# Expert sums gathered from the output, added on VectorE and scattered back, in place of an accumulating scatter into a scratch

## The chip, the core and the metric

The kernel runs on one core of a Trainium2 chip. The metric is device time in microseconds (us) of one execution, the median of some runs; lower is better. Engines are named as in the profile: PE is TensorE, DVE is VectorE, ACT is ScalarE, POOL is GpSimd, SP is SyncE. SPq and POOLq are instructions that these engines issue to the DMA engines.

## The reference

One layer of a diffusion backbone over 1024 tokens of 1024 channels: three mixers, a merge into the residual stream, and then a mixture of 16 experts with two experts for each token. Only its end is touched by the change. With `x` the stream after the mixers and `h2` its normalised and modulated copy:

```
x = x + g1 * merge_branches(...)
h2 = modulate(x, norm2_w, sh2, sc2)
expert, gate = route(h2, router_w, router_bias)        # two experts of a token, weights that sum to 1
y[e] = (silu(h @ w_gate[e]) * (h @ w_up[e])) @ w_down[e]   # for the tokens of expert e
out = x + g2 * sum over the two experts of (gate * y[expert])
```

All tensors are float32. Each expert has three 1024x1024 matrices, 12 MB, so the stage reads 192 MB of weights.

## The kernel before, in words

The stages run one after the other: the mixers, `project_out` (output projection, residual `x1`, second norm, router scores), `route` (which token sits in which slot) and `experts`. A block is 32 tokens of one expert; an expert has at least two blocks, and with these inputs there are 73. `k.block_row` holds the row numbers of each block. Empty slots of an expert's last block point at spare rows behind the 1024 real ones.

A block's data lies as 128 partitions of 256 columns: a token's row is cut into four quarters, and partition 32 j + r holds quarter j of slot r. So one indirect DMA of GpSimd moves 128 rows of 1 KB, each to or from a place of its own in DRAM.

`project_out` writes `x1` to the scratch tensor `sum_rows` (L2267) and the normalised rows to `xn_rows`; both scratch tensors have 32 spare rows, which are filled once (L2271). In `experts`, for block b:

- GpSimd gathers the block's rows of `xn_rows` into `rows` (L2574), ahead of their use.
- VectorE turns and modulates them into `rowsT` (`turn_rows`, L2583 to L2586).
- TensorE forms gate and up products (`p_gate_up`, L2697), then, for the block before, the down product (`p_y`, L2711).
- ScalarE and VectorE form the hidden values and turn them (`hide`, L2734 to L2753).
- VectorE scales `p_y` by the token's weight and by g2 into `y` (`store`, L2761), and counts it in the semaphore `y_stored`. TensorE's next `p_y` waits for that count.
- GpSimd scatters `y` with an accumulating indirect DMA: each row is added to its row of `sum_rows` (L2664). It counts in `added`. The next block's scatter and the next write of `y` wait for it, since two blocks may add to the same token.

SyncE streams the weights into a ring of 20 units of 1 MB (two half units of 512 KB); an expert needs 12. A unit is loaded again once the last block of its expert has used it (`gate_ups` and `downs` against the end of the expert), so loads come in bursts as an expert ends. All these queues share the 16 DMA engines.

When all scatters have landed, `finish` copies `sum_rows` to the output with four DMAs of 1 MB (L2792).

Of the kernel before, what the change touches and what calls it, by code (L numbers as in the profile page):

```python
# [22 lines left out]
F32 = mybir.dt.float32  # L23
# [2201 lines left out]
def project_out(k):  # L2225
# [4 lines left out]
    with ExitStack() as st:  # L2230
# [25 lines left out]
        with nc.Block() as block:  # L2256
            @block.sync
            def _(sp):
                credit(s, sp, per, "load_x", "load_x1_out", "load_xn_out")
                with sp.Fori(0, SEQ // P) as it:  # L2260
                    ps = Pass(s, sp, it, per)
                    src = dr["x"][0, ds(it * P, P), :]
                    d1, dn = dr["sums"][ds(it * P, P), :], dr["xn"][ds(it * P, P), :]
                    ps.after_last("x1")
                    sp.dma_start(x[:], src).then_inc(s("load_x"), 16)
                    ps.after("x1")
                    sp.dma_start(d1, x1[:]).then_inc(s("load_x1_out"), 16)  # L2267
                    ps.after("in_quarters")
                    sp.dma_start(dn, xq[:]).then_inc(s("load_xn_out"), 16)
                for name in ("sums", "xn"):  # L2270
                    sp.dma_start(dr[name][SEQ:SEQ + BLK, :], dr["x"][0, 0:BLK, :]).then_inc(s("spare_rows"), 16)  # L2271
                sp.wait_ge(s("load_x1_out"), 16 * (SEQ // P + 1))
                sp.wait_ge(s("load_xn_out"), 16 * (SEQ // P + 1))
                sp.wait_ge(s("spare_rows"), 32)
# [327 lines left out]
def experts(k):  # L2602
# [4 lines left out]
    with ExitStack() as st:  # L2607
# [8 lines left out]
        y = k.sb(st, "y", [P, W])  # L2616
        p_gu = k.ps(st, "p_gate_up", [P, 512])
        p_y = k.ps(st, "p_y", [P, 512])

        def quarters(name):  # L2620
            return dr[name].rearrange("t (i n) -> (t i) n", i=4)
# [10 lines left out]
        with nc.Block() as block:  # L2632
# [16 lines left out]
            def _(pool):  # L2649
# [6 lines left out]
                def add_rows(b):  # L2656

                    if not isinstance(b, int) or b:
                        pool.wait_ge(s("added"), b * 16)
                    nc.gpsimd.tensor_copy(row_y[:, :], k.block_row[:, ds(b, 1)]).then_inc(s("row_y"), 1)  # L2660
                    pool.wait_ge(s("row_y"), b + 1)
                    pool.wait_ge(s("y_stored"), b + 2)
                    pool.sem_inc(s("adds_begun"), 1)
                    nc.gpsimd.indirect_dma_start(quarters("sums"), bass.IndirectOffsetOnAxis(ap=row_y[:, 0:1], axis=0),  # L2664
                                                 y[:, :], None, compute_op=ALU.add).then_inc(s("added"), 16)

                n = blocks(pool)
                for b in (1, 2, 3):
# [3 lines left out]
                with pool.Fori(2, n) as b:  # L2672
                    pool.wait_ge(s("x_taken"), b + 2)
                    gather(b + 2)
                    add_rows(b + -1)
                add_rows(last_block(pool))
                pool.wait_ge(s("gathered"), pool.snap(n * 16 + 32))
                pool.wait_ge(s("added"), pool.snap(n * 16))
                pool.sem_inc(s("all_added"), 1)
# [57 lines left out]
            def _(dve):  # L2737
                ch = Chain(dve, s("dve_steps"))
                dve.sem_inc(s("hidden"), 1)  # L2739
# [15 lines left out]
                def store(b, ch):  # L2755

                    dve.wait_ge(s("downs"), b * 4 + 8)
                    if not isinstance(b, int) or b:
                        dve.wait_ge(s("added"), b * 16)
                    ch.run(nc.vector.tensor_copy(weight[:, :], k.block_weight[:, ds(b, 1)]))  # L2760
                    nc.vector.scalar_tensor_tensor(y[:, :], p_y[:, 0:W], weight[:, 0:1], g2[:, :], ALU.mult, ALU.mult) \  # L2761
                        .then_inc(s("y_stored"), 1)
# [8 lines left out]
                with dve.Fori(2, n) as b:  # L2771
                    ch.enter(b + -2, 3)
# [5 lines left out]


def finish(k):  # L2780

    nc, dr = k.nc, k.dram
    PARTS = 4
    with ExitStack() as st:
        s = Signals(nc, st, "fin")
        with nc.Block() as block:
            @block.sync
            def _(sp):
                sp.wait_ge(k.exp_signals("all_added"), 1)
                for n in range(PARTS):  # L2790
                    rows = slice(SEQ // PARTS * n, SEQ // PARTS * (n + 1))
                    sp.dma_start(dr["out"][0, rows, :], dr["sums"][rows, :]).then_inc(s("out"), 16)  # L2792
                sp.wait_ge(s("out"), 16 * PARTS)
# [49 lines left out]
def build(nc, dram):  # L2843
    k = Core(nc, dram)
    scratch(nc, dram)
    with ExitStack() as st:
# [24 lines left out]
        with ExitStack() as st_experts:  # L2871
# [8 lines left out]
            finish(k)  # L2880


def scratch(nc, dram):

    dram["sums"] = nc.dram_tensor("sum_rows", (SEQ + BLK, D), F32, kind="Internal").ap()
# [19 lines left out]
```

## Time and profile before

| what | value |
|---|---|
| median of 3 runs | 2865.71 us (2860.67 to 2866.39) |
| the profiled execution, its time | 2864.54 us |
| the profiled execution, its span | 2862.7 us |
| mean granted TensorE clock | 0.949 of full speed |
| busy share of the span | PE 90%, DVE 44%, ACT 20%, POOL 17% |
| indirect DMAs of the stage | 75 gathers, 73 scatters |
| memory traffic | 299.63 MB read, 22.50 MB written |

The span is the time from the first to the last instruction of the profiled execution, and its own time, 1.8 us more, is what compares with the runs. Times in the rows below are microseconds from the start of the span. The expert stage begins near 2062 and its last product ends near 2835. A row of a timeline has start, duration, engine, line of the kernel, operation, output <- inputs and in brackets the idle time of the engine before it with what ended it.

### The profile page before, as it was taken

What the parts mean: (1) busy time and instruction counts of PE and PEld (TensorE: products, weight loads), DVE (VectorE), ACT (ScalarE), POOL (GpSimd) and SP (SyncE); (2) the same over time, 40 slices, a digit from 0 to 9 for tenths busy, and PEclk for the clock granted to TensorE, in tenths of its full rate; (3) what the DMA queues carried; (4) which work ended last, traced back from release to release, by engine and by line L of the source; (5) the groups of instructions that cost most, each with busy time, mean ns of one, the idle gap of its engine ahead of it and who ended that gap; (6) DMA issues with size and microseconds to landing.
All of it is one profiled execution on the core that took longest, in us unless ns stands there. A gap on an engine that the chain in (4) does not pass through costs nothing. (4 is left out here: it accounts for less than half of the span.)

```text
span 2862.7 us, 57067 instructions
## 1 busy us (share of the span) xinstructions
PE 2588.4 (90%) x23169; PEld 1366.0 (48%) x23169; DVE 1261.7 (44%) x2179; ACT 568.6 (20%) x1080; POOL 474.1 (17%) x711
## 2 busy tenths in 40 slices
PE   5999858888898788799999999999499999999995
PEld 3444447776444466644444444445244444333442
DVE  2466656664764488504884211125422222222221
ACT  4333222322221377600000110013100000000000
POOL 0011145552111000000000000000023332233222
PEclk7999968999999999999999999999699999999998
DMA  6011010000010000030222231112677899869532
GB/s 236 22 30 36 1 47 11 19 19 31 22 44 0 15 1 1 1 81 26 81 74 77 73 100 59 34 52 95 236 295 268 336 377 400 331 226 352 202 85 77
DMA packets 198512, 320.17 MB, mean 112 GB/s; under 512 B 13601, under 2 KB 135944, under 8 KB 198120
## 3 DMA queue, kind: packets, MB, share of 16 engines
q1 hardware_dynamic: 183175, 294.11, 28.3%
q0 software_dynamic: 15168, 23.60, 3.7%
q8 instruction: 132, 2.16, 0.3%
q14 instruction: 37, 0.30, 0.0%
HBM read 299.63 MB, written 22.50 MB: 113 GB/s over the span
## 5 line engine op out<-in xcount | busy, mean ns | idle before, releaser
L2697 PE MATMUL p_gate_up<-w_unit,rowsT 128*32 128x512 f32 x4672 | 521.7, 597 | 17.6 <-DVEq L2739 8.1
L2034 PE MATMUL p_gate<-hT,w_gate 128*128 128x512 f32 x768 | 341.9, 598 | 6.5 <-DVE region L2158 5.3
L2697 PEld LDWEIGHTS p_gate_up<-w_unit,rowsT 128*32 128x32 f32 x4672 | 162.9, 111 | 331.1 <-issue 304.5
L2711 PE MATMUL p_y<-w_unit,hiddenT 128*32 128x256 f32 x4672 | 268.0, 381 | 1.2 <-DVE hiddenT L2753 1.2
L1080 PE MATMUL p_w<-hT,w_c 128*128 128x512 f32 (+1 forms) x640 | 248.7, 550 | 0.0
L2583 DVE STREAM_TRANSPOSE rows_turned<-rows 128x256 f32<-128x256 f32 x74 | 33.0, 445 | 452.3 <-PE p_gate_up L2697 447.5
L2034 PEld LDWEIGHTS p_gate<-hT,w_gate 128*128 128x128 f32 x768 | 144.0, 191 | 182.3 <-issue 180.7
L2711 PEld LDWEIGHTS p_y<-w_unit,hiddenT 128*32 128x32 f32 x4672 | 163.2, 111 | 123.7 <-issue 44.6
L1080 PEld LDWEIGHTS p_w<-hT,w_c 128*128 128x128 f32 x640 | 121.5, 190 | 124.9 <-issue 121.6
L2734 ACT ACTIVATE sigmoid<-p_gate_up 128x256 f32<-128x256 f32 x73 | 28.2, 386 | 746.0 <-PE p_gate_up L2697 746.0
L2183 DVE SCALAR_TENSOR_TENSOR region<-gated,taps,region x120 | 154.1, 1284 | 16.0
L2664 POOL DMA_INDIRECT sum_rows<-y,rows_to_add x73 | 117.6, 1611 | 150.7 <-DVE y L2761 144.0
L1996 POOL DMA_DIRECT2D half_region<-in_w_out x1 | 1.1, 1102 | 814.8 <-PE p_branch L2039 814.8
L2158 DVE TENSOR_TENSOR product<-p_branch,gate 128x512 f32<-128x512 f32 x32 | 22.1, 691 | 226.9 <-PE p_branch L2039 226.3
L941 DVE TENSOR_REDUCE part_max<-p_scores 128x1 f32<-128x512 f32 (+2 forms) x128 | 105.6, 825 | 36.2 <-PE p_scores L806 30.4
L806 PE MATMUL p_scores<-region 64*128 64x512 f32 (+1 forms) x384 | 84.3, 575 | 26.3 <-ACT p L885 24.8
L2098 ACT ACTIVATE gate<-p_gate 128x512 f32<-128x512 f32 x48 | 28.6, 596 | 358.4 <-PE p_gate L2034 358.4
L830 PE MATMUL p_out<-region,aT 128*128 128x128 f32 x640 | 80.9, 282 | 13.0 <-ACT aT L872 12.7
L885 ACT ACTIVATE p<-p_scores,minus_max 128x1280 f32<-128x1280 f32 x64 | 84.9, 1327 | 26.3 <-DVE minus_max L946 25.8
L1221 DVE SCALAR_TENSOR_TENSOR conv<-raw,head_taps,conv 128x1284 f32<-128x1284 f32 (+1 forms) x48 | 89.0, 1854 | 1.7
L674 DVE RECIPROCAL rinv<-root 128x512 f32<-128x512 f32 (+1 forms) x20 | 60.5, 3025 | 63.2 <-ACT root L609 63.2
L2574 POOL DMA_INDIRECT rows<-xn_rows,rows_to_gather x75 | 74.8, 997 | 62.7 <-POOL rows_to_gather L2652 60.1
(368 smaller groups left out, 3528.3 us busy)
## 6 DMA issues: line engine op xcount, KB each, us to landing
w_unit<-in_w_gate SPq DMA_DIRECT2D x128, 512.0 KB, 14.9
w_unit<-in_w_up SPq DMA_DIRECT2D x128, 512.0 KB, 16.5
w_unit<-in_w_down SPq DMA_DIRECT2D x128, 512.0 KB, 11.7
w_b<-in_w_mod SPq DMA_DIRECT2D x32, 512.0 KB, 3.9
w_gate<-in_w_in SPq DMA_DIRECT2D x24, 512.0 KB
region<-in_w_mod SPq DMA_DIRECT2D x4, 2048.0 KB, 14.7
w_c<-in_w_in SPq DMA_DIRECT2D x16, 512.0 KB
w_branch<-in_w_branch SPq DMA_DIRECT2D x24, 256.0 KB, 4.1
```

The lines of the kernel that those rows point to most:

```text
L806: mm = nc.tensor.matmul(score(m, at, size), k.qT[rows, h, q * P:q * P + P], k.kT[rows, h, at:at + size], start=True, stop=True)
L830: last = nc.tensor.matmul(p_o[:, 0:P], aT[:, t * P:(t + 1) * P], k.v[:, t, h * P:(h + 1) * P], start=(t == 0), stop=(t == NKT - 1))
L885: nc.scalar.activation(pm[m][j % (3 - m)][:, :], score(m, 0, TOK), ACT.Exp, bias=nb[:, 2 * (j % 2) + m:2 * (j % 2) + m + 1], scale=SCALE, ...
L941: ch.run(nc.vector.tensor_reduce(to, ap, AX.X, ALU.max))
L1080: last = nc.tensor.matmul(p_w[i % 5][:, 0:size], w[n][:, c, :], k.hT[:, c, at:at + size], start=(c == 0), stop=(c == KD - 1))
L1221: ins = nc.vector.scalar_tensor_tensor(dst, src[:, t:t + size], taps(n)[:, t:t + 1], dst, ALU.mult, ALU.add)
L2034: last = nc.tensor.matmul(p_g[half][:, :], wg[i][:, c, :], k.hT[:, c, CTX + at:CTX + at + 512], start=(c == 0), stop=(c == KD - 1))
L2183: ins = nc.vector.scalar_tensor_tensor(o, shifted(t), taps[:, t:t + 1], o, ALU.mult, ALU.add)
L2574: k.nc.gpsimd.indirect_dma_start(k.xg[:, :], None, k.dram["xn"].rearrange("t (i n) -> (t i) n", i=4), bass.IndirectOffsetOnAxis(ap=k.row_x ...
L2664: nc.gpsimd.indirect_dma_start(quarters("sums"), bass.IndirectOffsetOnAxis(ap=row_y[:, 0:1], axis=0), y[:, :], None, compute_op=ALU.add).t ...
L2697: last = nc.tensor.matmul(p_gu[part, :].rearrange("p (m c r) -> p m c r", m=2, r=BLK), xT[:, c, :], unit[:, :, j], start=(c == 0), stop=(c ...
L2711: last = nc.tensor.matmul(p_y[part, 0:W], hT[:, c, :], k.ring[u % UNITS][:, c % 2, W * j:W * j + W], start=(c == 0), stop=(c == KD - 1))
```

## The change

`x1` is written to the output itself, and `sum_rows`, its spare rows and `finish` go. For each block GpSimd now does three indirect DMAs: it fetches the block's present rows of the output into `rows_so_far`, gathers the rows of a later block as before, and scatters the finished sums. VectorE adds `rows_so_far` to `y` after it has scaled it. The scatter is a plain write. Fetch and scatter carry a bound on the row number, and rows beyond it (the empty slots) are skipped; `rows_so_far` is cleared once, so that skipped slots hold something. The fetch of a block waits for the landing of the scatter of the block before (`added`); VectorE's add waits for the fetch (`fetched`).

```
-                    d1, dn = dr["sums"][ds(it * P, P), :], dr["xn"][ds(it * P, P), :]
+                    d1, dn = dr["out"][0, ds(it * P, P), :], dr["xn"][ds(it * P, P), :]
...
-                for name in ("sums", "xn"):
-                    sp.dma_start(dr[name][SEQ:SEQ + BLK, :], dr["x"][0, 0:BLK, :]).then_inc(s("spare_rows"), 16)
+                sp.dma_start(dr["xn"][SEQ:SEQ + BLK, :], dr["x"][0, 0:BLK, :]).then_inc(s("spare_rows"), 16)
...
-                def add_rows(b):
+                def fetch_rows(b):
 
                     if not isinstance(b, int) or b:
                         pool.wait_ge(s("added"), b * 16)
+                        pool.wait_ge(s("y_stored"), b + 1)
                     nc.gpsimd.tensor_copy(row_y[:, :], k.block_row[:, ds(b, 1)]).then_inc(s("row_y"), 1)
                     pool.wait_ge(s("row_y"), b + 1)
+                    pool.sem_inc(s("fetches_begun"), 1)
+                    nc.gpsimd.indirect_dma_start(so_far[:, :], None, out_quarters,
+                                                 bass.IndirectOffsetOnAxis(ap=row_y[:, 0:1], axis=0),
+                                                 bounds_check=4 * SEQ - 1, oob_is_err=False).then_inc(s("fetched"), 16)
+
+                def add_rows(b):
+
                     pool.wait_ge(s("y_stored"), b + 2)
                     pool.sem_inc(s("adds_begun"), 1)
-                    nc.gpsimd.indirect_dma_start(quarters("sums"), bass.IndirectOffsetOnAxis(ap=row_y[:, 0:1], axis=0),
-                                                 y[:, :], None, compute_op=ALU.add).then_inc(s("added"), 16)
+                    nc.gpsimd.indirect_dma_start(out_quarters, bass.IndirectOffsetOnAxis(ap=row_y[:, 0:1], axis=0),
+                                                 y[:, :], None, bounds_check=4 * SEQ - 1, oob_is_err=False) \
+                        .then_inc(s("added"), 16)
 
                 n = blocks(pool)
+                pool.wait_ge(s("cleared"), 1)
+                fetch_rows(0)
                 for b in (1, 2, 3):
                     pool.wait_ge(s("x_taken"), b)
                     gather(b)
                 add_rows(0)
                 with pool.Fori(2, n) as b:
+                    fetch_rows(b + -1)
                     pool.wait_ge(s("x_taken"), b + 2)
                     gather(b + 2)
                     add_rows(b + -1)
+                fetch_rows(last_block(pool))
                 add_rows(last_block(pool))
...
+                nc.vector.memset(so_far[:, :], 0.0).then_inc(s("cleared"), 1)
...
                     ch.run(nc.vector.tensor_copy(weight[:, :], k.block_weight[:, ds(b, 1)]))
-                    nc.vector.scalar_tensor_tensor(y[:, :], p_y[:, 0:W], weight[:, 0:1], g2[:, :], ALU.mult, ALU.mult) \
-                        .then_inc(s("y_stored"), 1)
+                    ch.run(nc.vector.scalar_tensor_tensor(y[:, :], p_y[:, 0:W], weight[:, 0:1], g2[:, :], ALU.mult,
+                                                          ALU.mult))
+                    dve.wait_ge(s("fetched"), b * 16 + 16)
+                    nc.vector.tensor_tensor(y[:, :], y[:, :], so_far[:, :], ALU.add).then_inc(s("y_stored"), 1)
...
-def finish(k):
...
-                sp.wait_ge(k.exp_signals("all_added"), 1)
-                for n in range(PARTS):
-                    rows = slice(SEQ // PARTS * n, SEQ // PARTS * (n + 1))
-                    sp.dma_start(dr["out"][0, rows, :], dr["sums"][rows, :]).then_inc(s("out"), 16)
-                sp.wait_ge(s("out"), 16 * PARTS)
```

GpSimd's program in the loop over blocks, before (the ISA, REGISTER_ALU and branch rows are waits and loop control; line numbers of each kernel are its own):

```order
L2652 ISA
L2652 COPY rows_to_gather<-block_rows 128x1
L2653 REGISTER_ALU
L2574 DMA rows<-xn_rows,rows_to_gather 128x256
L2659 ISA
L2660 ISA
L2660 COPY rows_to_add<-block_rows 128x1
L2662 REGISTER_ALU
L2664 DMA sum_rows<-y,rows_to_add 4224x256
```

and the same loop in the changed kernel:

```order
L2660 ISA
L2660 COPY rows_to_add<-block_rows 128x1
L2663 DMA rows_so_far<-out,rows_to_add 128x256
L2684 REGISTER_ALU
L2651 ISA
L2651 COPY rows_to_gather<-block_rows 128x1
L2652 REGISTER_ALU
L2573 DMA rows<-xn_rows,rows_to_gather 128x256
L2669 REGISTER_ALU
L2671 DMA out<-y,rows_to_add 4096x256
```

The copy of the row numbers moved from behind the gather to the head of the loop, where it waits for the last scatter's landing, and the fetch follows it; the gather now stands behind the fetch.

VectorE's `store` in its loop over blocks, before:

```order
L2757 ISA
L2759 REGISTER_ALU
L2760 REGISTER_ALU
L2760 COPY weight<-block_weights 128x1
L194 REGISTER_ALU
L2761 SCALAR_TENSOR_TENSOR y<-p_y,weight,g_quarters 128x256
L2771 REGISTER_ALU
L2771 COMPARE_AND_BRANCH
```

and in the changed kernel:

```order
L2769 ISA
L2771 REGISTER_ALU
L2772 REGISTER_ALU
L2772 COPY weight<-block_weights 128x1
L194 REGISTER_ALU
L2773 SCALAR_TENSOR_TENSOR y<-p_y,weight,g_quarters 128x256
L194 REGISTER_ALU
L2775 REGISTER_ALU
L2776 TENSOR_TENSOR y<-y,rows_so_far 128x256
L2785 REGISTER_ALU
L2785 COMPARE_AND_BRANCH
```

`y_stored` is now counted by the add (L2776), which has a wait for the fetch ahead of it. After it the loop comes round to `turn_rows` of a later block.

## Rows read from the trace of the kernel before

**Rows 1.** The page, parts 1 and 2: busy time; busy tenths in 40 slices.
```profile
PE 2588.4 (90%) x23169; PEld 1366.0 (48%) x23169; DVE 1261.7 (44%) x2179; ACT 568.6 (20%) x1080; POOL 474.1 (17%) x711
...
DMA  6011010000010000030222231112677899869532
```

**Rows 2.** Waits from 1980 on: engine, line, waited for; us, times, longest us.
```profile
POOL rows_to_add L2660 <- DMA sum_rows<-y,rows_to_add: 20.2, 23, 2.3
...
PE p_gate_up L2697 <- DMA w_unit<-in_w_up: 7.2, 5, 2.2
...
DVE rows_turned L2583 <- DMA rows<-xn_rows,rows_to_gather: 4.8, 1, 4.8
```

**Rows 3.** Timeline of one block while the DMA engines are idle.
```profile
2785.14 3.64 PE L2711 MATMUL p_y<-w_unit,hiddenT 128*32 128x256 f32 x64
...
2787.23 0.42 DVE L2750 TENSOR_TENSOR hidden<-p_gate_up,sigmoid 128x256 f32<-128x256 f32 x1
2787.28 1.00 POOL L2574 DMA_INDIRECT rows<-xn_rows,rows_to_gather  x1 [0.83 <-POOL rows_to_gather L2652]
2788.27 0.20 POOL L2660 COPY rows_to_add<-block_rows 128x1 int32 x1
...
2789.35 0.48 DVE L2761 SCALAR_TENSOR_TENSOR y<-p_y,weight,g_quarters 128x256 f32<-128x256 f32 x1
...
2790.69 1.61 POOL L2664 DMA_INDIRECT sum_rows<-y,rows_to_add  x1 [2.21 <-DVE y L2761]
...
2795.45 3.64 PE L2711 MATMUL p_y<-w_unit,hiddenT 128*32 128x256 f32 x64
```

**Rows 4.** Timeline of the last two scatters, and the output's rows of the scratch.
```profile
2831.97 1.61 POOL L2664 DMA_INDIRECT sum_rows<-y,rows_to_add  x1 [2.21 <-DVE y L2761]
...
2835.89 0.18 POOL L2660 COPY rows_to_add<-block_rows 128x1 int32 x1 [2.30 <-DMA sum_rows<-y,rows_to_add]
...
2837.37 1.59 POOL L2664 DMA_INDIRECT sum_rows<-y,rows_to_add  x1 [1.30 <-DVE y L2761]
...
L2792 SPq DMA_DIRECT2D out<-sum_rows x4: 578/586/589, 2845.9 to 2847.8; - x4
...
DMA to landing us min/median/max: 2.6/2.6/13.3
```

**Rows 5.** Timeline of the first two gathers and the turns that follow them.
```profile
2052.76 1.04 POOL L2574 DMA_INDIRECT rows<-xn_rows,rows_to_gather  x1 [0.93 <-POOL rows_to_gather L2503]
...
2063.26 0.99 POOL L2574 DMA_INDIRECT rows<-xn_rows,rows_to_gather  x1 [0.84 <-POOL rows_to_gather L2652]
...
2058.87 0.45 DVE L2583 STREAM_TRANSPOSE rows_turned<-rows 128x256 f32<-128x256 f32 x1 [4.79 <-DMA rows<-xn_rows,rows_to_gather]
...
2071.87 0.45 DVE L2583 STREAM_TRANSPOSE rows_turned<-rows 128x256 f32<-128x256 f32 x1 [8.98 <-PE p_gate_up L2697]
```

**Rows 6.** GB/s in 40 slices, from 2786.5 to 2790.5 and from 2790 to 2795.
```profile
GB/s 0 0 0 0 0 0 0 0 0 0 0 0 0 0 0 0 0 0 0 0 0 0 0 0 164 205 287 164 164 205 287 0 0 0 0 0 0 0 0 0
...
GB/s 0 0 0 0 0 0 0 0 0 0 0 0 0 0 0 0 0 0 0 0 0 0 8 106 57 131 164 147 164 148 74 41 8 0 0 0 0 0 0 0
```

**Rows 7.** Timeline of one scatter while weights stream.
```profile
2170.86 1.61 POOL L2664 DMA_INDIRECT sum_rows<-y,rows_to_add  x1 [2.21 <-DVE y L2761]
...
2180.34 0.18 POOL L2660 COPY rows_to_add<-block_rows 128x1 int32 x1 [1.58 <-DMA sum_rows<-y,rows_to_add]
```

**Rows 8.** Windows: length, busy of each engine, then granted clock, DMA share, GB/s.
```profile
2107.90:2784.00 676.10, 668.94 (x8240) 286.08 (x8236) 194.36 (x513) 24.69 (x64) 202.72 (x257) 0.99 0.79 293
2283.40:2492.80 209.40, 205.19 (x2488) 88.13 (x2484) 57.63 (x153) 7.32 (x19) 61.25 (x77) 0.98 1.01 386
2703.00:2769.10 66.10, 66.10 (x840) 27.17 (x836) 20.99 (x56) 2.61 (x7) 20.43 (x27) 1.00 0.15 26
2420.00:2440.00 20.00, 16.43 (x164) 5.20 (x157) 3.02 (x8) 0.38 (x1) 4.17 (x5) 0.83 1.04 409
```

**Rows 9.** Timeline of TensorE, the `p_y` group behind the longest wait for weights.
```profile
2428.97 5.56 PE L2711 MATMUL p_y<-w_unit,hiddenT 128*32 128x256 f32 x64
```

More of the change, by code:

```diff
@@ L2269, in _ @@
                     sp.dma_start(dn, xq[:]).then_inc(s("load_xn_out"), 16)
-                for name in ("sums", "xn"):
-                    sp.dma_start(dr[name][SEQ:SEQ + BLK, :], dr["x"][0, 0:BLK, :]).then_inc(s("spare_rows"), 16)
+                sp.dma_start(dr["xn"][SEQ:SEQ + BLK, :], dr["x"][0, 0:BLK, :]).then_inc(s("spare_rows"), 16)
                 sp.wait_ge(s("load_x1_out"), 16 * (SEQ // P + 1))
                 sp.wait_ge(s("load_xn_out"), 16 * (SEQ // P + 1))
-                sp.wait_ge(s("spare_rows"), 32)
+                sp.wait_ge(s("spare_rows"), 16)
             @block.gpsimd
@@ L2616, in experts @@
         y = k.sb(st, "y", [P, W])
+        so_far = k.sb(st, "rows_so_far", [P, W])
         p_gu = k.ps(st, "p_gate_up", [P, 512])
         p_y = k.ps(st, "p_y", [P, 512])
-        def quarters(name):
-            return dr[name].rearrange("t (i n) -> (t i) n", i=4)
+        out_quarters = dr["out"].rearrange("a t (i n) -> (a t i) n", i=4)
         def blocks(eng):
@@ L2678, in _ @@
                 pool.wait_ge(s("added"), pool.snap(n * 16))
-                pool.sem_inc(s("all_added"), 1)
             @block.tensor
@@ L2771, in _ @@
                 with dve.Fori(2, n) as b:
-                    ch.enter(b + -2, 3)
+                    ch.enter(b + -2, 4)
                     dve.wait_ge(s("gate_ups"), b * KD + 2 * KD)
@@ L2777, in _ @@
                 store(last_block(dve), Chain(dve, s("dve_last_steps")))
-def finish(k):
[L2782 to L2788, printed above, removed]
-                sp.wait_ge(k.exp_signals("all_added"), 1)
-                for n in range(PARTS):
-                    rows = slice(SEQ // PARTS * n, SEQ // PARTS * (n + 1))
-                    sp.dma_start(dr["out"][0, rows, :], dr["sums"][rows, :]).then_inc(s("out"), 16)
-                sp.wait_ge(s("out"), 16 * PARTS)
 INPUTS = ["x", "c", "ctx", "c_ctx", "w_mod", "b_mod", "norm1_w", "norm2_w", "w_in", "qn_w", "kn_w", "lam_p", "subln_w",
@@ L2879, in build @@
             experts(k)
-            finish(k)
 def scratch(nc, dram):
-    dram["sums"] = nc.dram_tensor("sum_rows", (SEQ + BLK, D), F32, kind="Internal").ap()
     dram["decay_rows"] = nc.dram_tensor("decay_rows", (TOK // P * 8, 2, P), F32, kind="Internal").ap()
```

## The prediction

> **What bounds the kernel now.** I read the page first: TensorE is busy nearly all of the span, and the busy share of the DMA engines shows that the last third, the expert stage, is where they are full [rows 1]. Then the waits of that stage: TensorE waits only 7.2 us for weights; GpSimd's copy of a block's row numbers waits 23 times, up to 2.3 us, for the scatter of the block before [rows 2]. Then one block while the DMA engines have little to do [rows 3]. The reader is to see TensorE going from one group of products to the next without a gap: 10.31 us lie between the starts of two `p_y` groups (2785.14 and 2795.45). VectorE writes y from 2789.35 to 2789.83, GpSimd starts the scatter at 2790.69, 0.86 us later, and TensorE needs that y to be written only when it starts the next `p_y` at 2795.45. So y has 5.6 us to spare, and TensorE waits for no scatter. The stage is TensorE's. After it come the last scatter, the copy to the output and the end [rows 4].
>
> **The copy at the end.** The last scatter starts at 2837.37. The one before it was answered 3.9 us after its start (2831.97 to 2835.89), so the last lands near 2841.3 [rows 4]. SyncE issues the copy from 2845.9 on, 4.6 us later. The last of its four issues starts at 2847.8, the slowest lands 13.3 us after its issue, near 2861.1, and the span ends at 2862.7. The 4.6 us stay, since GpSimd still has to end its block, and so do the 1.6 us of closing. What goes is 2862.7 - 2841.3 - 4.6 - 1.6 = 15.2 us. Nothing covers this copy, so the gain is whole. The small copy into the spare rows of `sum_rows` lay beside VectorE's routing and is worth nothing.
>
> **What is added, by block.** GpSimd gets a fetch and VectorE an add of the size of its other 128x256 products, 0.42 us. Engine time is no trouble: GpSimd gets about 2.0 us a block (copy 0.20, wait 0.83, a gather's issue 1.00) and VectorE 0.4, both in idle time [rows 3]. The memset (about another 0.42 us) and the first fetch put the gather of block 1 some 2.6 us later: issued at 2063.26 before, now 2065.9, landed near 2072.0 at a price of 6.1 us, where VectorE begins with it at 2071.87, after its wait for TensorE [rows 5]. That is 0.1 us, nothing.
>
> What costs is the order in time. Before, a scatter waited for the scatter before it, and that was all. Now each block's fetch waits for the landing of the scatter before, the add for the fetch, and the scatter for the add: a closed loop through two DMA landings, which must turn once a block. TensorE waits for it by `y_stored`; VectorE stands in `store`, with the next `turn_rows` and `hide` behind it; GpSimd's gather is behind the fetch. The loop is y to scatter start 0.86, landing of the scatter, copy 0.20 and wait 0.83, landing of the fetch, add 0.42: 2.31 us and two landings.
>
> **The landings.** With idle DMA engines, the gather issued at 2787.28 moves its last bytes near 2789.6, 2.3 us later, and the accumulating scatter issued at 2790.69 near 2794.1, 3.4 us later; such a scatter is answered after 3.9, so 0.5 behind its bytes [rows 3, 4, 6]. A gather then takes about 2.8, and I take 2.9 with the waiting engine's reaction. With a plain scatter at the same price the loop is 2.31 + 5.8 = 8.1 us, below 10.31: no wait, and 2.2 us in hand.
>
> While weights stream, landings are longer: the first gather, issued at 2052.76, released VectorE at 2058.87, 6.1 us later [rows 5], and the scatter issued at 2170.86 released GpSimd at 2180.34, after 9.5 us [rows 7]. The 23 waits say the same: in a smooth block the copy stands 7.9 us behind the scatter before it (10.31 less the 2.42 from 2788.27 to 2790.69), so a wait means over 7.9 us [rows 2, 3]. For the fetch I take the gather's 6.1. The plain scatter is in no row; its bounds are the quiet 2.9 below and the loaded accumulate's 9.5 above. It moves a gather's bytes and doesn't read the sum, so it is nearest the gather; I take 6.5, a little over it, for the writing of 128 separate rows. The 288 empty slots of 73 x 32 = 2336 (2048 are used) are 12% of a small transfer: nothing. The loaded loop is then 2.31 + 6.5 + 6.1 = 14.9 us, 4.6 more than TensorE's 10.31.
>
> The Trainium skill, page "DMA: Bandwidth & Descriptors", section "Anatomy of one DMA", gives a DMA issued by GpSimd about 2.0 us plus its bytes over 436 GB/s, which makes an estimated 2.3 us for 128 KB, with no term for what else runs. By that the loop stays below TensorE's block, and the sum would be that of the third rival below. The quiet rows are near it, the loaded rows (6.1 and 9.5 us) are not.
>
> **How long it is loaded.** From 2107.9 to 2784.0 the DMA share is 0.79; a loaded stretch has 1.01, a quiet one 0.15 [rows 8]. So loaded time is (0.79 - 0.15)/(1.01 - 0.15) = 74% of 676.1 us, 503 us, and the bytes set it. The ring holds 20 of the 192 units, so 172 come in this stretch, in 14.3 bursts of 12, as experts give up their units. A DMA issued in about the last 5 us of a burst finds the queue nearly empty (my choice, a little under a loaded landing): 503 - 14.3 x 5 = 431 us count.
>
> - In them the loop turns 431/14.9 = 28.9 times, each 4.6 us late: +133 us.
> - The other 65.5 - 28.9 = 36.6 blocks of the stretch (676.1/10.31 = 65.5) run quiet, and each makes up 2.2 us: 81. But y can be no more than 5.2 us ahead (5.6 less the add), and four long quiet stretches of 23 to 66 us (138 us, 13.4 blocks; the longest is in rows 8) could make up 29 and have 4 x 5.2 = 21 to make up. So -73.
> - Weights that were late are there when TensorE is late: -7 [rows 2].
> - The tail: the last block's loop is quiet and TensorE is done. From 2831.97: add 0.42, landing 2.9, copy and wait 1.03, landing 2.9, add 0.42, start 0.86, landing 2.9 gives 2843.4 in place of 2841.3: +2. The copy: -15.
>
> Sum: 133 - 73 - 7 + 2 - 15 = +40 us. The profiled execution took 2864.5 us (span 2862.7), which makes 2905; the median of the runs is 1.2 above the profiled one, within their spread. One doubt: in a stretch with a granted clock of 0.83 (a mean between the levels of 1.2 and 2.4 GHz), behind the longest wait for weights, 2.2 us, a `p_y` group took 5.56 us in place of 3.64 [rows 2, 3, 8, 9]. Longer waits may lower the clock too; a late block leaves TensorE 4.6 us idle, which covers as much, so I add nothing.
>
> **The rivals.**
> 1. The plain scatter lands as late as the accumulate, about 8.5 us loaded (between 7.9 and 9.5) and 3.9 quiet. The loop is 16.9 loaded and 9.1 quiet: 431/16.9 = 25.5 turns, 6.6 late each, +168; the other 40 make up 1.2 each, -48; -7; tail 4 - 15 = -11. That is +102, 2967. For it: both write 128 separate rows. Against it: the longer issue of the accumulate (1.61 against 1.00 us) is the add's. A fetch that took 8.2 us comes to nearly the same; it can't be more, since a gather has 8.2 us from its issue to TensorE's next `p_y` (2787.28 to 2795.45), and VectorE waited for one only once [rows 2, 3].
> 2. The plain scatter lands as in quiet, 2.9, since the stream reads from memory and this writes. The loop is 11.3, 1.0 late on 38 blocks, +38; the quiet ones make up all but some 5 to 15, and with the tail it ends even, 2855 to 2867. Against it: the accumulate lost over 4 us to the stream.
> 3. The other side: beside the weights these DMAs land nearly as in quiet, and the loaded accumulates were slow for a reason of their own. It decides where the two landings together stay under 10.31 - 2.31 = 8.0 us. Then only the end counts: 2 - 15, 2852. For it: the quiet rows. Against it: 6.1 of the 8.0 go to one gather [rows 5].
>
> **How the numbers follow.** My forecast (2880 to 2935 by itself) 0.66, rival 1 0.17, rival 2 0.07, rival 3 0.10. The range reaches from the middle of rival 2 to just over rival 1, 2860 to 2972, and leaves out rival 3, half of rival 2 and the far end of rival 1. About 0.2% is what this measurement tells from no change. Faster: rival 3 and 0.01 of rival 2, 0.11; same: 0.04; slower: 0.85.
>
> **What would show it.** In the profile after, TensorE's `p_y` waits for VectorE's y, over 50 us in all and only in loaded stretches; VectorE's add waits for the DMA into `rows_so_far`; GpSimd's copy of row numbers waits for the scatter in nearly every loaded block; such blocks are 13 to 16 us apart, quiet ones 10.3; the stretch from the last `p_y` to the end is some 13 us shorter. I am wrong if loaded blocks stay at 10.3 us (one of the two landings is then well under 6 us beside the weights), or if quiet blocks are late too (a quiet landing is over 4 us).

## The result

The changed kernel takes 2946.85 us (median of 4 runs, 2941.99 to 2947.58); the kernel before, run beside it, 2863.19 (4 runs, 2858.91 to 2866.39). The ratio is 1.0281, 95% interval 1.0257 to 1.0304: slower, by 84 us. The profiled execution took 2947.58 us, its span is 2945.7, the granted clock 0.946.

The page after, parts 1 and 2 (the rows that answer to [rows 1]):

```profile
PE 2612.2 (89%) x23169; PEld 1393.7 (47%) x23169; DVE 1292.6 (44%) x2253; ACT 568.2 (19%) x1080; POOL 496.1 (17%) x784
...
DMA  6111010001010000202222221024859679558521
```

Busy shares hardly moved, and no engine is new at the top. The waits did. Those of the changed kernel from 2000 us on, the rows that answer to [rows 2] (columns as there):

```profile
DVE y L2776 <- DMA rows_so_far<-out,rows_to_add: 240.4, 49, 7.0
POOL rows_to_add L2660 <- DMA out<-y,rows_to_add: 239.3, 72, 6.6
POOL out L2671 <- DVE y L2776: 228.4, 68, 4.9
...
DVE rows_turned L2582 <- DMA rows<-xn_rows,rows_to_gather: 66.0, 37, 9.4
...
PE p_y L2722 <- issue: 71.1, 33, 4.5
...
DVE weight L2772 <- DMA out<-y,rows_to_add: 40.2, 24, 3.3
```

Three waits of about 230 to 240 us, on GpSimd for the scatter, on VectorE for the fetch and on GpSimd for y, are one loop seen from its three corners. TensorE, which waited for no y before, now stands 71.1 us in front of `p_y`. The view calls it "issue" (no releaser found), but the timeline of a turn beside the stream shows what came just ahead of it:

```profile
2174.82 1.01 POOL L2671 DMA_INDIRECT out<-y,rows_to_add  x1 [3.07 <-DVE y L2776]
...
2182.26 0.19 POOL L2660 COPY rows_to_add<-block_rows 128x1 int32 x1 [6.43 <-DMA out<-y,rows_to_add]
...
2183.35 1.05 POOL L2663 DMA_INDIRECT rows_so_far<-out,rows_to_add  x1 [0.90 <-POOL rows_to_add L2660]
...
2189.23 0.42 DVE L2776 TENSOR_TENSOR y<-y,rows_so_far 128x256 f32<-128x256 f32 x1 [5.56 <-DMA rows_so_far<-out,rows_to_add]
...
2190.58 1.01 POOL L2671 DMA_INDIRECT out<-y,rows_to_add  x1 [4.19 <-DVE y L2776]
...
2203.76 0.43 DVE L2776 TENSOR_TENSOR y<-y,rows_so_far 128x256 f32<-128x256 f32 x1 [5.95 <-DMA rows_so_far<-out,rows_to_add]
...
2204.28 5.14 PE L2722 MATMUL p_y<-w_unit,hiddenT 128*32 128x256 f32 x64 [3.38 <-issue]
```

The scatter at 2174.82 is answered after 7.4 us (the copy at 2182.26), the fetch at 2183.35 after 5.9 (the add at 2189.23), and the next scatter starts 15.8 us after the first. `p_y` starts 0.1 us after the add at 2203.76 has ended. Between two bursts of the stream, with little on the DMA engines, the same turn fits:

```profile
2738.03 3.66 PE L2722 MATMUL p_y<-w_unit,hiddenT 128*32 128x256 f32 x64
...
2744.22 1.01 POOL L2671 DMA_INDIRECT out<-y,rows_to_add  x1 [3.07 <-DVE y L2776]
2746.83 0.18 POOL L2660 COPY rows_to_add<-block_rows 128x1 int32 x1 [1.59 <-DMA out<-y,rows_to_add]
2747.91 1.04 POOL L2663 DMA_INDIRECT rows_so_far<-out,rows_to_add  x1 [0.90 <-POOL rows_to_add L2660]
...
2748.35 3.66 PE L2722 MATMUL p_y<-w_unit,hiddenT 128*32 128x256 f32 x64
...
2753.20 0.42 DVE L2776 TENSOR_TENSOR y<-y,rows_so_far 128x256 f32<-128x256 f32 x1
2754.54 1.01 POOL L2671 DMA_INDIRECT out<-y,rows_to_add  x1 [3.07 <-DVE y L2776]
```

Here the scatter is answered after 2.6 us, the add waits for nothing in its row, and `p_y` groups stand 10.32 us apart.

**Where the 83 us of the span are.** I cut the span at the first and the last scatter. The view of the scatter's line gives both; for before, and for after with its landings:

```profile
L2664 POOL DMA_INDIRECT sum_rows<-y,rows_to_add x73: 1588/1611/1643, 2088.4 to 2837.4; - x73
```
```profile
L2671 POOL DMA_INDIRECT out<-y,rows_to_add x73: 1010/1014/1032, 2085.6 to 2933.0; - x73
...
DMA to landing us min/median/max: 2.3/4.1/7.5
```

From the first scatter to the last: 749.0 us before, 847.4 after, +98.4. From the last scatter to the end of the span: 25.3 and 12.7, -12.6. Ahead of the first scatter: -2.8. Together +83.0. The last part can't be put down to the change: over the profiled executions told of here the first scatter starts anywhere from 2083.1 to 2096.6. So below I compare the stretch between the scatters and the end, and the medians only beside them.

The 98.4 us by turns, from the 72 distances between scatter starts in the timeline: 37 are longer than 10.6 us, 518.9 us together, mean 14.0, which is 137 more than 37 x 10.31. 20 are shorter than 10.0 and win back 32; 15 are TensorE's 10.31. The net, 105, less the 6.7 by which the 749.0 us of before are over 72 x 10.31, is 98.

The same 98.4 us by TensorE, from windows over that stretch, before and after (length, busy of each engine, then clock, DMA share, GB/s):

```profile
2088.40:2837.40 749.00, 738.15 (x9136) 317.02 (x9128) 215.95 (x570) 27.39 (x71) 225.00 (x287) 1.00 0.74 269
```
```profile
2085.60:2933.00 847.40, 768.37 (x9131) 352.30 (x9120) 248.57 (x642) 27.29 (x71) 247.52 (x358) 0.97 0.63 246
```

TensorE stands still 79 us in place of 11, 68 more, and it is busy 30 us longer for the same products, at a mean granted clock of 0.97 in place of 1.00, 1.00 being its level of 2.4 GHz.

### The profile page after: what moved, and what is told of

Same layout as the page of the kernel before. It is cut to its first block and busy times, and to the rows that moved or that the text cites. A ratio compares the mean times of both kernels' runs of the same rounds, so it can differ in the third digit from the quotient of the medians.

```text
span 2945.7 us, 57622 instructions
## 1 busy us (share of the span) xinstructions
PE 2612.2 (89%) x23169; PEld 1393.7 (47%) x23169; DVE 1292.6 (44%) x2253; ACT 568.2 (19%) x1080; POOL 496.1 (17%) x784
## 5 line engine op out<-in xcount | busy, mean ns | idle before, releaser
L2708 PE MATMUL p_gate_up<-w_unit,rowsT 128*32 128x512 f32 x4672 | 520.7, 597 | 13.8 <-DVEq L2751 8.0
L2722 PE MATMUL p_y<-w_unit,hiddenT 128*32 128x256 f32 x4672 | 292.2, 405 | 71.1 <-issue 71.1
L2708 PEld LDWEIGHTS p_gate_up<-w_unit,rowsT 128*32 128x32 f32 x4672 | 175.3, 111 | 316.5 <-issue 303.3
L2722 PEld LDWEIGHTS p_y<-w_unit,hiddenT 128*32 128x32 f32 x4672 | 185.3, 117 | 200.6 <-issue 142.0
L2776 DVE TENSOR_TENSOR y<-y,rows_so_far 128x256 f32<-128x256 f32 x73 | 31.0, 425 | 243.3 <-DMA rows_so_far<-out,rows_to_add 240.4
L2671 POOL DMA_INDIRECT out<-y,rows_to_add x73 | 74.0, 1014 | 234.0 <-DVE y L2776 228.4
L830 PE MATMUL p_out<-region,aT 128*128 128x128 f32 x640 | 80.9, 282 | 13.0 <-ACT aT L872 12.8
```

The source lines that it names most:

```text
L830: last = nc.tensor.matmul(p_o[:, 0:P], aT[:, t * P:(t + 1) * P], k.v[:, t, h * P:(h + 1) * P], start=(t == 0), stop=(t == NKT - 1))
L2671: nc.gpsimd.indirect_dma_start(out_quarters, bass.IndirectOffsetOnAxis(ap=row_y[:, 0:1], axis=0), y[:, :], None, bounds_check=4 * SEQ - 1, ...
L2708: last = nc.tensor.matmul(p_gu[part, :].rearrange("p (m c r) -> p m c r", m=2, r=BLK), xT[:, c, :], unit[:, :, j], start=(c == 0), stop=(c ...
L2722: last = nc.tensor.matmul(p_y[part, 0:W], hT[:, c, :], k.ring[u % UNITS][:, c % 2, W * j:W * j + W], start=(c == 0), stop=(c == KD - 1))
```

## The experiments

What each kernel's profiled execution showed, from the scatter's line and the span (the median is of its runs; the kernel before had medians of 2861.04 to 2865.33 beside them):

| kernel | median us | first scatter | first to last scatter | last scatter to end |
|---|---|---|---|---|
| before | 2863.19 | 2088.4 | 749.0 | 25.3 |
| after | 2946.85 | 2085.6 | 847.4 | 12.7 |
| accumulate into the output | 2845.99 | 2083.1 | 745.9 | 9.3 |
| loop in the scratch | 2967.88 | 2090.3 | 842.2 | 28.4 |
| fetch unbound | 2853.08 | 2093.4 | 744.9 | 12.6 |
| row numbers ahead | 2943.18 | 2092.3 | 832.2 | 12.8 |
| after, no stream | 2845.02 | 2089.6 | 740.9 | 12.8 |
| before, no stream | 2852.79 | 2085.8 | 738.1 | 25.1 |
| skip only | 2861.66 | 2096.6 | 745.7 | 25.1 |
| longer loop | 2973.36 | 2091.2 | 866.4 | 12.8 |
| plain scatter alone | 2842.36 | 2089.6 | 739.6 | 6.6 |
| idle fetch | 2859.13 | 2096.2 | 750.4 | 11.5 |
| half the stream | 2878.52 | 2094.9 | 770.8 | 12.7 |

My theory: the loop of two landings, long only beside the weight stream, costs what it is longer than TensorE's 10.31 us. The rivals are that the DMAs themselves, their target, the skipping, or TensorE's clock cost it.

**The end part alone: accumulate into the output.**

```
-nc.gpsimd.indirect_dma_start(quarters("sums"), bass.IndirectOffsetOnAxis(ap=row_y[:, 0:1], axis=0),
-                             y[:, :], None, compute_op=ALU.add).then_inc(s("added"), 16)
+nc.gpsimd.indirect_dma_start(out_quarters, bass.IndirectOffsetOnAxis(ap=row_y[:, 0:1], axis=0),
+                             y[:, :], None, bounds_check=4 * SEQ - 1, oob_is_err=False,
+                             compute_op=ALU.add).then_inc(s("added"), 16)
...
-finish(k)
```

> The accumulating scatter of before, but straight into the output with empty slots skipped, no fetch, no add, no copy at the end. My theory (the change lost its time in the closed loop of scatter, fetch and add; its end part alone is a gain): TensorE's p_y groups stay 10.31 us apart as before, and only the end changes, by the 15.2 us worked out from the rows of before: 2863.2 - 15.2 = 2848 us (2845 to 2853). Rival A (scatters into the output tensor, or the skipping, are what is slow): scatters land later than the 8.0 us loaded and 3.9 us quiet of before, TensorE waits for y, and the time is above 2863. Rival B (the end costs the same without the copy, because GpSimd's end of block was the bound): 2860 to 2864.

2845.99 us (5 runs), ratio 0.9931 (0.9918 to 0.9945): faster than both kernels. First to last scatter 745.9, as before, and the end is 25.3 - 9.3 = 16.0 shorter, where I had 15.2. GpSimd's waits for the scatter are those of before:

```profile
POOL rows_to_add L2658 <- DMA out<-y,rows_to_add: 15.6, 14, 2.4
```

Neither the output as the target nor the end of the change costs anything. Rivals A and B fall.

**The loop alone, in the scratch.** The change with `sum_rows` as its target and the copy at the end.

```
-out_quarters = dr["out"].rearrange("a t (i n) -> (a t i) n", i=4)
+out_quarters = dr["sums"].rearrange("t (i n) -> (t i) n", i=4)
...
+finish(k)
```

> The fetch, add and plain scatter of the change, but on the scratch of sums and with the copy at the end put back: the loop alone. My theory: the loop costs what it cost in the changed kernel. p_y of block 0 to p_y of block 71 took 743.7 us before and 839.5 after, +96; the copy back gives some 10 to 13 us more than the changed kernel's 2946.9: 2957 to 2960 us. Rival A (it is the output tensor that makes the landings long): with the scratch as target the landings of scatter and fetch fall well below 6 us beside the weights, and the time is under 2920.

2967.88 us, ratio 1.0362 (1.0347 to 1.0378). The stretch is 842.2 us, +93 over before, so the loop is slow wherever its rows are. The median is 8 us over my bound. The span, 2960.9, is 15.2 over the changed kernel's: the end 15.7, the first scatter 4.7, the stretch -5.2; what remains lies between its runs (2962.72 to 2971.47).

**The fetch taken out of the loop.** It reads rows of `xn` with row numbers of its own and doesn't wait for the scatter, so the output gets other rows than the sums so far; the scatter itself waits for the scatter before it (`added`) instead. DMAs, bytes and products stay.

```
 def fetch_rows(b):
-    pool.wait_ge(s("added"), b * 16)
     pool.wait_ge(s("y_stored"), b + 1)
...
-    nc.gpsimd.indirect_dma_start(so_far[:, :], None, out_quarters,
-                                 bass.IndirectOffsetOnAxis(ap=row_y[:, 0:1], axis=0),
+    nc.gpsimd.indirect_dma_start(so_far[:, :], None, xn_quarters,
+                                 bass.IndirectOffsetOnAxis(ap=row_f[:, 0:1], axis=0),
```

> The changed kernel, but the fetch reads the same rows of xn instead of the output, with row numbers of its own, and so is issued without waiting for the scatter before it. The same DMAs, bytes and engine work stay; what is added to the output are other rows than the sums so far. My theory (the time goes into the chain of two landings, not into the DMAs themselves): the loop is y to scatter 0.92, one landing of at most 7.4 us, product and add 0.9, under 10.31, so TensorE is late in no block; 2946.9 less the 96 us of the stage, 2850 us (2847 to 2860). Rival A (the extra 128 KB a block and the busy GpSimd queue slow weights, gathers and TensorE): the stage stays long, 2900 us or more. Rival B (half and half, for instance because two small DMAs in flight land later than one): between 2865 and 2900, with waits of VectorE's add for rows_so_far of over 30 us.

2853.08 us, ratio 0.9952 (0.9935 to 0.9969), stretch 744.9. VectorE's wait for the fetch, 240.4 us in the changed kernel, is gone:

```profile
DVE y L2784 <- DMA rows_so_far<-xn_rows,rows_to_fetch: 2.2, 4, 1.0
```

With every DMA still there, the loss is gone as soon as one landing no longer follows the other. The fetch reads another tensor too, but that is not what helps: gathers from `xn_rows` that stand in the changed kernel's chain of waits land after 5.4 and 6.4 us beside the stream (2267.24 and 2592.22), as its fetches do. So the chain costs it, not the traffic.

**No stream beside the stage**, in the changed kernel and in the one before: the 172 weight units beyond the ring aren't loaded, and stale weights are used.

```
-load_unit(k, sp, u)
+sp.sem_inc(s("unit_loaded", u % UNITS), 32)
```

> The changed kernel with the 172 weight units beyond the ring's 20 not loaded (the signals that they are there are given at once), so that nothing streams beside the experts' stage; the weights used are stale. My theory (the landings are long only beside the stream): the loop turns in about 7.9 us, less than TensorE's 10.31, so from p_y of block 0 to p_y of block 71 it takes 71 x 10.31 = 732 us; the time is 732 - 839.5 from the changed kernel's 2946.9, 2840 us (2835 to 2850), and under the kernel before with the same cut by what the end gives, 10 to 15 us. Rival A (the loop is too long by itself, whatever streams): over 2900 us, and longer than the kernel before with the same cut.

> The kernel before with the same cut: the 172 weight units beyond the ring's 20 not loaded, stale weights used. It is what the run above is held against. The stage from p_y of block 0 to p_y of block 71 should go from 743.7 us to 71 x 10.31 = 732, so 2863 - 12 = 2851 us (2846 to 2856) by every theory; if the loop does no harm without the stream, the changed kernel with this cut is 10 to 15 us below it.

2845.02 us for the changed kernel, 2852.79 for the one before: without the stream the change is a gain of 7.8 us, less than the 10 to 15 I had. The loop's stretch is 740.9 us, 732.7 of them to the 72nd scatter, as worked out. It is 2.8 over the stretch of the kernel before with the same cut, and nearly all of that is the last turn (8.2 us against 5.5); the first scatter is 3.8 later and the end 12.3 shorter. All 72 copies still stand behind a scatter's landing, but briefly:

```profile
POOL rows_to_add L2660 <- DMA out<-y,rows_to_add: 118.6, 72, 4.5
```

A mean of 1.6 us in place of 3.3, and VectorE waits for the fetch 3.8 us in all, in 3 blocks. Rival A falls: nothing in the loop is too long by itself.

**A shorter loop: row numbers ahead.** The fetch gets its own tile, copied before the scatter lands, so that neither the copy nor a wait for it stands between the landing and the fetch.

```
 def fetch_rows(b):
-    pool.wait_ge(s("added"), b * 16)
     pool.wait_ge(s("y_stored"), b + 1)
-    nc.gpsimd.tensor_copy(row_y[:, :], k.block_row[:, ds(b, 1)]).then_inc(s("row_y"), 1)
-    pool.wait_ge(s("row_y"), b + 1)
+    nc.gpsimd.tensor_copy(row_f[:, :], k.block_row[:, ds(b, 1)]).then_inc(s("row_f"), 1)
+    pool.wait_ge(s("row_f"), b + 1)
+    pool.wait_ge(s("added"), b * 16)
```

> The changed kernel, but the fetch has its own tile of row numbers, copied before the scatter has landed, so that the copy (0.20 us) and the wait behind it (0.83 us) leave the loop and nothing else changes. My theory: every one of the 37 turns longer than TensorE's 10.31 us is shorter by 1.0 us (mean 14.0 to 13.0), -37 us, and quiet turns win back a little more: 2946.9 - 37 = 2910 us (2900 to 2917). Rival A (TensorE is late because of its lower clock, or of DMA contention, not by the length of the loop): 2940 or more. Rival B (the landing takes the time back, because a fetch issued earlier waits longer behind the weights): 2925 to 2947, with fetch landings of over 6.5 us.

2943.18 us, ratio 1.0278 (1.0262 to 1.0294): my number was wrong, and the median lies in the ranges of both rivals. The chain of waits of this kernel shows why, at its last fetch:

```profile
2916.80 2.66 DMA out<-y,rows_to_add
2919.46 0.02 issue
2919.48 0.02 POOLq L2664
2919.50 0.06 issue
2919.56 0.03 POOLq L2665
2919.59 0.75 issue
2920.34 2.81 DMA rows_so_far<-out,rows_to_fetch
```

The copy is gone and 0.88 us still lie between landing and fetch. What I had read as a wait for the copy is time GpSimd takes ahead of an indirect DMA in any case. In the late turns of the changed kernel the distance is 1.22 (2197.02 to 2198.24 in its chain of waits), so the edit took out 0.34 us, not 1.03. For that the loop theory gives 37 x 0.34 = 13 us and a little won back, and the stretch went from 847.4 to 832.2, -15. The sum fits, but not turn by turn: the late turns have nearly the same mean, 14.1 us, and there are 34 of them, 128 us over TensorE's, while the short ones win back 38. The median landing of the scatter is 4.6 us in place of 4.1, so the landings seem to have taken part of the 0.34 back, as rival B has it, though of the 21 fetches beside the stream in its chain of waits only 2 took over its 6.5 us. This run alone does not show what the length of the loop costs. The first scatter started 6.7 us later than in the changed kernel, which hid half of it in the time.

**A longer loop.** Two further additions of zeros to y on VectorE.

```
-nc.vector.tensor_tensor(y[:, :], y[:, :], so_far[:, :], ALU.add).then_inc(s("y_stored"), 1)
+ch.run(nc.vector.tensor_tensor(y[:, :], y[:, :], so_far[:, :], ALU.add))
+ch.run(nc.vector.tensor_tensor(y[:, :], y[:, :], zeros[:, :], ALU.add))
+nc.vector.tensor_tensor(y[:, :], y[:, :], zeros[:, :], ALU.add).then_inc(s("y_stored"), 1)
```

> The changed kernel with two further VectorE additions of a tile of zeros to y behind the addition of the sums so far: the loop becomes longer by about 0.95 us a turn (two products of 0.42 and their waits on one another), and nothing else. The run with the row numbers ahead took 0.33 us out of the loop, not the 1.0 that I had expected (0.89 us stay between a scatter's landing and the fetch's start with no copy there), and its stretch from the first scatter to the 72nd went from 839.5 to 824.5 us. My theory (each turn beside the stream costs TensorE what it is longer than 10.31 us): some 37 turns are longer by 0.95 us, +35, and the quiet turns win back less, 20 turns by up to 0.95 each, +19: the stretch from the first scatter to the 72nd takes 875 to 895 us, the time 2980 to 3000. Rival A (the late blocks come from the DMAs' own contention or from TensorE's clock, and the length of the loop says little): under 2960.

```profile
2196.01 0.42 DVE L2778 TENSOR_TENSOR y<-y,rows_so_far 128x256 f32<-128x256 f32 x1 [5.68 <-DMA rows_so_far<-out,rows_to_add]
2196.47 0.42 DVE L2779 TENSOR_TENSOR y<-y,zeros 128x256 f32<-128x256 f32 x1
2196.93 0.42 DVE L2780 TENSOR_TENSOR y<-y,zeros 128x256 f32<-128x256 f32 x1
```

Each turn is 0.92 us longer, but the time is 2973.36 us (ratio 1.0388, 1.0367 to 1.0409), +27, and the stretch +19: over rival A's bound, under mine. I had kept 37 late turns. There are 32, of mean 15.0 (480.6 us together, 151 over TensorE's); 26 short ones win back 30. TensorE, later, gives up weight units later, and quiet turns appear between bursts: from 2213 to 2263 the turns were 9.7, 15.6, 15.1 and 8.9 us, where the changed kernel had 12.9, 14.8, 12.0, 13.4 and 13.8 from 2205 to 2272. So a longer loop cost more a turn and had fewer such turns; that it is the later TensorE which makes the quiet turns is read from this stretch.

**Half the stream.** Half of every row of the 172 units is loaded, the other half is stale.

```
+part = slice(0, D if u < UNITS else D // 2)
-eng.dma_start(k.ring[u % UNITS][:, half, :], src)
+eng.dma_start(k.ring[u % UNITS][:, half, part], src[:, part])
```

> The changed kernel with half of each of the 172 streamed weight units loaded (half of every row; the other half is stale), so that half the bytes stream beside the stage. From the first scatter to the last took 847.4 us with the whole stream and 740.9 with none. My theory (landings stay as long while a burst lasts, there is half as much loaded time, and between bursts y wins back its lead, which it could do in only 8 places in the changed kernel): the late turns cost about half of 137 us, 68, and some 14 quiet gaps win back up to 3.7 each, 25 to 50: 760 to 785 us from the first scatter to the last, and 2946.9 - 75 = 2872 us (2858 to 2887). Rival A (nothing more is won back between bursts; the loss goes with the bytes): half of 106.5, 794 us, and 2893. Rival B (with half the bytes the landings shorten, so that two of them fit under 10.31 us): under 748 us, and 2840 to 2850.

2878.52 us (ratio to before 1.0047, 1.0029 to 1.0066), stretch 770.8: inside my bounds, outside both rivals'. The late turns are 68 us over TensorE's, half of 137, and the short ones win back 38. The landings are nearly as long at most, 6.6 us, but half are quick:

```profile
DMA to landing us min/median/max: 2.3/2.5/6.6
```

So the loss goes with the loaded time, less what quiet turns win back. It does not need a lower clock either. The window over this stretch (columns as above) has a granted clock of 1.00:

```profile
2094.90:2865.70 770.80, 741.20 (x9130) 353.40 (x9120) 247.84 (x642) 27.23 (x71) 249.30 (x359) 1.00 0.45 153
```

**Skipping alone**: the kernel before with its accumulate bounded.

```
-y[:, :], None, compute_op=ALU.add)
+y[:, :], None, bounds_check=4 * SEQ - 1, oob_is_err=False, compute_op=ALU.add)
```

> The kernel before with one part of the change alone: its accumulating scatter into the scratch of sums skips the empty slots by a bounds check. My theory: skipping 288 of 2336 small rows is worth nothing, as TensorE waits for no scatter: 2861 to 2868 us, no change. Rival A (the check or the skipped rows make the scatter land later, past y's 5.6 us in hand): over 2870. Rival B (fewer packets free the DMA queues for weights): under 2858.

2861.66 us, ratio 0.9992 (0.9980 to 1.0005): nothing, as expected.

**The end of GpSimd's block.** From its last scatter to its end the changed kernel took 12.7 us, the accumulate into the output 9.3, though its scatter lands later. Two kernels ask what does it: a plain scatter without fetch or add (sums are left out), and the accumulate with a fetch that nothing uses.

```
-oob_is_err=False, compute_op=ALU.add).then_inc(s("added"), 16)
+oob_is_err=False).then_inc(s("added"), 16)
```

> The run that accumulates into the output, but with a plain scatter in place of the accumulating one, so that rows are overwritten and the sums are left out; no fetch, no add. It asks two things. First the end: from the start of the last scatter to the end of the span took 9.3 us with the accumulate alone and 12.7 us in the changed kernel, whose last scatter itself landed sooner. Theory A (GpSimd's end of block takes longer the more indirect DMAs it has issued; 146 in this kernel as with the accumulate alone, 219 in the changed one): with a landing of 2.5 in place of 3.9 us the end takes 7.9 us. Theory B (plain scatters are what makes the end of the block long): 11 to 13 us. Second the landing of a plain scatter without a fetch around it, beside the weights: if it is as in the changed kernel it lands after 5 to 7.5 us, and no block is late: 2843 to 2848 us in all.

```
 with pool.Fori(2, n) as b:
+    fetch_rows(b + -1)
     pool.wait_ge(s("x_taken"), b + 2)
```

> The run that accumulates into the output with the fetch of rows of xn added to it, issued ahead of the scatter and used by nothing (no add; the output is the reference's). It is 73 indirect DMAs more and no longer loop. Theory A for the end (it grows with the number of indirect DMAs): 9.3 + 3.3 = 12.6 us from the last scatter to the end, and the time is 2846.0 + 3.3, about 2849 us. Theory B (plain scatters make the end long): 9.3 us there, about 2846. If the traffic of the fetch alone costs TensorE anything, the stretch from the first scatter to the 72nd is over 745 us (740.4 with the accumulate alone), and the time is over 2853.

The plain scatter alone ends in 6.6 us (theory A had 7.9), so plain scatters aren't what is long. The idle fetch adds 2.2 to the accumulate's 9.3, and a fetch adds 6.0 to the plain scatter's 6.6 (12.6 with the fetch unbound). So the fetches make the end longer, as theory A has it, but not by one price per DMA; how they do stays open. The first kernel's 2842.36 us (ratio 0.9923, 0.9894 to 0.9952) were a little under my 2843 to 2848. The second's 2859.13 (0.9978, 0.9963 to 0.9993) miss the 2849 of theory A. The fetch's traffic is not clearly the reason: the stretch to the 72nd scatter is 743.5 us, under the 745 that I had set, against 740.4 with the accumulate alone, and to the last it is 4.5 us longer, while VectorE's y waits for the fetch 23.9 us in all. The rest is the first scatter, 13.1 us later in the profiled execution, which no theory here accounts for.

## Why the prediction was right, and what it mis-sized

I predicted 2905 us, +40; it is 2947, +84, inside a range of 2860 to 2972 that is wide. The way and the mechanism came out, the size was half of what it is. By its steps:

- **The closed loop is the cause.** Shown: cutting it (fetch unbound) or taking away what makes its landings long (no stream) removes the whole loss, with all else there.
- **The landings.** I took 6.5 and 6.1 us loaded, a loop of 14.9, and 8.1 quiet. The late turns have a mean of 14.0, the turn shown 15.8 with landings of 7.4 and 5.9, and quiet turns with y late 7.9 (2717.21 to 2725.15). The accumulate's 9.5 [rows 7] was indeed its own: plain scatters land after 2.3 to 7.5 us. The Trainium skill, page "DMA: Bandwidth & Descriptors", section "Anatomy of one DMA", has about 2.0 us plus bytes over 436 GB/s, an estimated 2.3 us here: the quiet 2.6 us are near it, the 7.4 us beside the stream are not, and the run without the stream shows that the stream makes the difference.
- **+133 for the late turns.** Measured 137, in part by luck: it is 37 turns of 3.7 us in place of 28.9 of 4.6. I read this as two errors that cancel. Turns only partly loaded are late too, but less (the shortest late one is 10.9 us), and the 5 us that I took off each of 14.3 bursts were too much where bursts run into each other.
- **-73 made up by quiet blocks: this step failed.** "The other 65.5 - 28.9 = 36.6 blocks of the stretch run quiet, and each makes up 2.2 us." It is 32. The count of quiet blocks was right, 35 turns beside the 37 late ones, but only 20 make up anything. y can win back no more than its lead, 5.2 us by my own sum, in one place, and the quiet turns lie together in 8 places that won back 3.0 to 4.5 us each. I had set that limit for four long quiet stretches and let the other quiet blocks stand between all 14.3 bursts. The trace of before says otherwise: bursts run into each other there already. Windows over it have a loaded stretch of 105 us and, behind a pause of 8.3, the one of 209.4 in [rows 8]:

```profile
2146.60:2169.90 23.30, 23.30 (x300) 11.65 (x296) 7.45 (x21) 0.77 (x2) 7.50 (x10) 1.00 0.16 28
2169.90:2275.10 105.20, 105.20 (x1304) 51.20 (x1300) 30.43 (x81) 3.84 (x10) 32.50 (x41) 1.00 1.01 385
2275.10:2283.40 8.30, 8.30 (x116) 4.26 (x109) 2.89 (x8) 0.38 (x1) 2.11 (x4) 1.00 0.20 32
```

  There are six pauses from 2107.9 to 2784.0 (from 2146.6, 2275.1, 2492.8, 2545.1, 2641.3 and 2703.0 on), and six times 5.2 us is 31. In the changed kernel eight late turns follow on one another from 2174.82 to 2285.75, with a DMA share of 0.91 from 2205.10 to 2272.02. That TensorE is late is not the reason: before, where it waited for no y, the stream had no pause from 2169.90 to 2275.10 either, and the longer loop, whose TensorE is later still, has more short turns, 26. With half the stream there is more room, and less loss needs more of it: 38 us won back of 68.
- **"So I add nothing" for the clock** was part of that. A block right behind a run of late ones is slow although the loop has already caught up. TensorE's timeline, and windows over such a block and a quiet one (length, busy of each engine, then clock, DMA share, GB/s):

```profile
2136.35 4.98 PE L2722 MATMUL p_y<-w_unit,hiddenT 128*32 128x256 f32 x64 [3.94 <-issue]
2141.14 7.05 PE L2708 MATMUL p_gate_up<-w_unit,rowsT 128*32 128x512 f32 x64
2148.01 3.64 PE L2722 MATMUL p_y<-w_unit,hiddenT 128*32 128x256 f32 x64
```
```profile
2136.00:2148.00 12.00, 11.65 (x128) 4.93 (x132) 3.69 (x10) 0.00 (x0) 4.42 (x6) 0.87 0.34 129
...
2738.00:2748.30 10.30, 10.30 (x132) 5.04 (x128) 3.44 (x9) 0.39 (x1) 3.54 (x6) 1.00 0.12 38
```

  Behind 3.94 us of standing still, `p_y` took 4.98 us in place of 3.66, at a mean granted clock of 0.87, between the levels of 1.2 and 2.4 GHz; the next `p_y` came 11.66 us later, while the loop turned in 7.9 (2146.92 to 2154.86). Six blocks read like this, 1.4 to 1.7 us each, 9.5 us that could otherwise have been won back. The other slow `p_y` groups of the timeline stand in late turns, where I take it that the loop sets the length anyway; so I don't count all of the 30 us above as lost. No run takes the clock alone out of the changed kernel, so this share is read, not shown.
- **The tail and the copy.** Mine came to -16 behind the last scatter (landing 2.9 in place of 3.9, no copy). The accumulate into the output, whose landing stays as it was, gave -16.0 where 15.2 were worked out for it; the changed kernel gave -12.6, since "the 4.6 us stay" of GpSimd's closing did not hold with the fetches.
- **Weights, skipping, gathers.** TensorE's waits for weights are gone from the list, as said. Skipping is worth nothing. Gathers behind the fetch are late 37 times (66.0 us), nearly always in a late turn or right behind one, and TensorE's `p_gate_up` waits for VectorE's rows and hidden values only 4.8 us in all.

Of the rivals, the first (2967) ends nearer to the measured time than my forecast, for the wrong reason: its plain scatter of 8.5 us loaded and 3.9 quiet is in no row. The second (a quick scatter beside the stream) and the third (both quick) are contradicted by the 7.4 and 5.9 us, and by what taking the stream away gives.

## What to carry to other kernels

A DMA that nobody waits for can be slow; before it is made one link of a read, add, write chain, put all its landings beside the tightest loop of the stage, at the price they have while everything else streams. Lateness that such a loop causes is won back only where the stream pauses, and in each pause no more than the loop's lead: so count the pauses in the trace, not the quiet time. The gain here was in the other half of the change: accumulating straight into the output, without the copy, takes 0.9931 of the time before.

## What the runs showed of the hardware that I had not expected

- GpSimd took 0.88 us from a landing to the next indirect DMA even where its indices had been copied before the landing, 0.75 of it "issue" (row numbers ahead).
- A plain indirect scatter of 128 KB is issued in 1.01 us and landed after 2.3 to 7.5 in the changed kernel; the accumulating one takes 1.61 to issue, and was answered after 3.9 us quiet and 9.5 loaded [rows 4, 7].
- From the last scatter to the end of the span it took longer with fetches, though the last of them had landed before that scatter: 12.6 us in place of 6.6 behind a plain scatter, 11.5 in place of 9.3 behind an accumulating one.
- Profiled executions of kernels that are nearly alike up to the expert stage reach its first scatter at 2083.1 to 2096.6 us; a few us between medians are best checked against a stretch of the trace.
